# Behind four norms: the fourth tile's high-weight products move between the last input rows of the first three tiles, and the splits and the last sum around them change places

## The chip, the cores and the metric

One core of a Trainium2 chip runs the whole program. The metric is the device time of one execution in microseconds (us). TensorE (PE) does the matrix products, VectorE (DVE) and ScalarE (ACT) the elementwise work, GpSimd (POOL) a part of the gated product of the feed-forward layers, and SyncE (SP) starts the loads of the weights from memory.

## The reference, cut to what matters

Two networks run one after the other on 256 tokens (the first with 16 extra ones in front, so 272 columns) of width 1024. The first one has a gated DeltaNet layer and an mLSTM layer, each followed by a convolutional feed-forward layer; the second one has a mixed convolution and attention layer, a mixed linear and latent attention layer, and two SwiGLU layers. What surrounds the change is this part, which stands behind each mixer and each feed-forward layer of the first network:

```python
def rms_norm(x, w):
    xf = x.astype(jnp.float32)
    y = xf * lax.rsqrt(jnp.mean(xf * xf, -1, keepdims=True) + RMS_EPS)
    return (y * w.astype(jnp.float32)).astype(x.dtype)
...
    hs = hs + keep * rms_norm(mix, norm_w[i, 1])
    f = conv_ffn(rms_norm(hs, norm_w[i, 2]), ffn_w_up[i], ffn_conv_w[i], ffn_conv_b[i], ffn_w_down[i])
    hs = hs + keep * rms_norm(f, norm_w[i, 3])
```

So a layer's output is normalised and added to `hs`, the new `hs` is normalised again, and the result is multiplied by the next weight matrix (the feed-forward layer's `w_up`, or a mixer's `w_in`).

## The kernel before, in words

**Weights.** All weight matrices lie in one stream of 399 blocks that are split, plus a few that are used as they are. A block is 128 x 1024: for a matrix of the "tiles" kind it holds the weights that give one tile of 128 output rows, as eight 128 x 128 pieces, one for each of the eight 128-row pieces of the input (KC = 8). Four slots (`SLOTS`) hold four blocks. SP loads block n into `raw` once block n-4 has been split. ACT makes the high half `whi`, a copy rounded to fp32r (`split_hi`, line 394); it waits for the load, and for PE to be done with block n-4 (`block_used`). DVE makes the low half `wlo` = `raw` - `whi` (`split_lo`, line 399). The input is kept in the same way as a high part, `xs[:, k]`, and a low part, `xs[:, 8 + k]`. A product of the two is three matmuls: high weight by high input, high weight by low input, low weight by high input (`three`, lines 421, 422 and 423). An output tile takes 8 x 3 = 24 of them, all into one of eight banks.

**The wave.** Where a phase begins behind a norm, the input arrives row by row, so `pe_tiles` works on the first three tiles (`AHEAD` = 3) at once. For k = 0 to 7 it takes, as soon as the high part of row k is there, six matmuls (line 440 and 441: both weight halves of three blocks by the high input), and one step later three more with the low input of the row before (line 447). Then it goes on tile by tile with 24 matmuls each (`tile`), each tile behind a wait for its `wlo` and for its bank.

**The norm's scale.** The mean square of `hs` isn't needed for these products: each output is multiplied by the scale afterwards. ACT squares each row (line 735), DVE adds the squares in pairs and fours (`pair_sum`, `four_sum`, lines 688 and 694), and PE adds the two fours over the partitions with a matrix of ones (line 626, through `meanwhile`: `four3` within step 6 and `four7` within step 8, in both cases before the three matmuls of line 447). Then ACT takes the logarithm (`act_scale`, line 546) and the exponential (line 549): that is the scale. Between the two it splits the fifth block's high half. Its next instruction loads the function table of the next phase (lines 3175, 1848 and 3187), and only after it the high half of the sixth block is split. DVE's first instruction of the feed-forward phase multiplies tile 0 by the scale (line 862), and it then waits for that high half to make the sixth block's low half, before it comes to tile 1.

**The four places.** `pe_tiles` is called with such a wave behind `post0` (phase `up0`, 44 tiles of 272 columns), `post1` (`ml_in`, the mLSTM's first 13 tiles of 272 columns), `post2` (`up1`, 44 tiles of 258 columns) and `post3` (`ev_in`, six tiles of 256 columns). The last one begins the second network, which has no norm there, so it has no squares, no sum and no scale. `next_act` and `next_dve` are ACT's and DVE's part at the first three places, `last_act` and `last_dve` at the fourth. In front of each wave PE does 16 matmuls whose results nobody reads (`keep_clock`, line 617).

In the mLSTM phase DVE's first work behind the scale is the sixth block's low half and the two gate rows; ACT waits for these, and DVE waits for ACT again before it begins two scans over the tokens (lines 1875 and 1876), with products and low halves between their steps. PE waits for what comes of them (line 2162) before it goes on at line 1974.

**Order.** Every engine works through its own instructions in the order in which they are written; semaphores alone tie them together. The order within `next_dve` and `next_act` is written out by hand.

Of the kernel before, what the change touches and what calls it, by code (L numbers as in the profile page):

```python
# [21 lines left out]
P = 128  # L22
D = 1024
KC = D // P
N_META, SEQ = 16, 256
T1 = N_META + SEQ
# [27 lines left out]
SLOTS = 4  # L54
AHEAD = 3
# [230 lines left out]
def build(nc, stream, params, consts, mla, hs_in, out, table):  # L286
# [15 lines left out]
    whi_f, whi = shared("whi_f", [P, SLOTS, BLOCK], "whi", [P, SLOTS, BLOCK])  # L302
    wlo_f, wlo = shared("wlo_f", [P, SLOTS, BLOCK], "wlo", [P, SLOTS, BLOCK])
# [33 lines left out]
    def splits(n):  # L337
        return n + 1 - (len(PLAIN) if n >= PLAIN.stop else 0)
# [6 lines left out]
    hi_split = sem("hi_split")  # L345
# [43 lines left out]
    def split_hi(act, n, i=0):  # L389
        s = n % SLOTS  # L390
        act.wait_ge(block_loaded[s], i * (16 * 8 // SLOTS) + 16 * (n // SLOTS + 1))
        if n >= SLOTS:
            act.wait_ge(block_used, i * 8 + (n - SLOTS + 1))
        nc.scalar.activation(whi[:, s, :], raw[:, s, :], ACT.Copy).then_inc(hi_split, 1)  # L394

    def split_lo(dve, n, i=0):
        s = n % SLOTS
        dve.wait_ge(hi_split, i * 8 + splits(n))
        nc.vector.tensor_tensor(wlo[:, s, :], raw[:, s, :], whi[:, s, :].bitcast(F32), ALU.subtract).then_inc(block_split, 1)  # L399

    def fourth(phase):
        return FIRST_BLOCK[phase] + AHEAD

    def fifth(phase):
        return FIRST_BLOCK[phase] + AHEAD + 1
# [16 lines left out]
        nc.tensor.matmul(out_, whi[:, slot, w], lo, start=False, stop=False)  # L422
        return nc.tensor.matmul(out_, wlo[:, slot, w], hi, start=False, stop=stop)  # L423

    def pe_tiles(pe, phase, g0, name, count=None, meanwhile=lambda k: None):

        b0, n = FIRST_BLOCK[phase], count or COUNT[phase]
        T = cols(phase)
        mm = nc.tensor.matmul

        for k in range(KC + 1):
            if k < KC:
                w = slice(k * P, (k + 1) * P)
                pe.wait_ge(*S("norm", "act").at(f"{name}_hi{k}"))
                for j in range(AHEAD):
                    o, s = rhs_out(g0 + j, phase), (b0 + j) % SLOTS
                    if k == 0:
                        pe.wait_ge(block_split, splits(b0 + j))
                        pe.wait_ge(bank_free, g0 + j + 1)
                    mm(o, whi[:, s, w], xs[:, k, T], start=(k == 0), stop=False)  # L440
                    mm(o, wlo[:, s, w], xs[:, k, T], start=False, stop=False)  # L441
            if k:
                meanwhile(k - 1)
                w = slice((k - 1) * P, k * P)
                pe.wait_ge(*S("norm", "dve").at(f"{name}_lo{k - 1}"))
                for j in range(AHEAD):
                    last = mm(rhs_out(g0 + j, phase), whi[:, (b0 + j) % SLOTS, w], xs[:, KC + k - 1, T], start=False, stop=(k == KC))  # L447
                    if k == KC:
                        last.then_inc(block_used, 1)

        def tile(j, i=0):
            g = g0 + j
            pe.wait_ge(block_split, i * 8 + splits(b0 + j))
            pe.wait_ge(bank_free, i * 8 + (g + 1))
            for k in range(KC):
                last = three(rhs_out(g, phase), (b0 + j) % SLOTS, k, xs[:, k, T], xs[:, KC + k, T], k == 0, k == KC - 1)
            last.then_inc(block_used, 1)

        turns = (n - AHEAD) // 8
        if turns:  # L460
            with pe.Fori(0, turns) as i:
                for j in range(AHEAD, AHEAD + 8):
                    tile(j, i)
        for j in range(AHEAD + turns * 8, n):
            tile(j)

    def width(phase):
# [14 lines left out]
    def rhs_out(g, phase):  # L482
        return bank[g % 8][:, cols(phase)]
# [59 lines left out]
    def act_scale(act, name, g, dst, T, count, eps, lo=0, meanwhile=lambda: None):  # L543

        act.wait_ge(*S("norm", "pe").at(name))
        nc.scalar.activation(dst, bank[g % 8][:, lo:T], ACT.Ln, bias=eps, scale=1.0 / count).then_inc(bank_free, 1)
        meanwhile()
        act.wait_ge(bank_free, 8 + g + 1)
        nc.scalar.activation(dst, dst, ACT.Exp, scale=-0.5).then_inc(*S("norm", "act").mark(f"{name}_scale"))
# [134 lines left out]
    def pair_sum(dve, name, m, T, lo=0):  # L684

        v = S("norm", "dve")
        dve.wait_ge(*S("norm", "act").at(f"{name}_{m}"))
        nc.vector.tensor_tensor(sq[:, m, lo:T], sq[:, m - 1, lo:T], sq[:, m, lo:T], ALU.add).then_inc(*v.mark(f"{name}_pair{m}"))
# [19 lines left out]
    def next_dve(dve, post, name, row, phase):  # L708
        t = slice(PRE_FIRST[name], T1)

        def lo(m):
            dve.wait_ge(*S("norm", "act").at(f"{name}_hi{m}"))
            nc.vector.scalar_tensor_tensor(xs[:, KC + m, t], hs[:, m, t], pv("norm_w", row * KC + m), xs[:, m, t].bitcast(F32),
                                           ALU.mult, ALU.subtract).then_inc(*S("norm", "dve").mark(f"{name}_lo{m}"))

        for m in range(KC):
            add_y(dve, post, m)
            if m:
                lo(m - 1)
            if m % 2 == 0 and m:  # L720
                pair_sum(dve, name, m - 1, T1, t.start)
            if m == 5:
                four_sum(dve, name, 3, T1, t.start)
        lo(KC - 1)
        pair_sum(dve, name, KC - 1, T1, t.start)
        four_sum(dve, name, KC - 1, T1, t.start)
        split_lo(dve, fourth(phase))
        split_lo(dve, fifth(phase))

    def next_act(act, post, name, row, g, phase):  # L730
        t = slice(PRE_FIRST[name], T1)
        for m in range(KC):
            act.wait_ge(*S("norm", "dve").at(f"{post}_h{m}"))
            nc.scalar.activation(xs[:, m, t], hs[:, m, t], ACT.Copy, scale=pv("norm_w", row * KC + m)).then_inc(*S("norm", "act").mark(f"{name}_hi{m}"))  # L734
            nc.scalar.activation(sq[:, m, t], hs[:, m, t], ACT.Square).then_inc(*S("norm", "act").mark(f"{name}_{m}"))
            if m == 4:
                split_hi(act, fourth(phase))
        act_scale(act, name, g, rs[:, 0, t], T1, D, eps_1, t.start, lambda: split_hi(act, fifth(phase)))

    def last_dve(dve, post, name):  # L740

# [2519 lines left out]
    @block.tensor  # L3261
    def _(pe):
        first_pe(pe, "pre0", G["pre0"])
        pe.wait_ge(loaded, 16)
        gates_pe(pe, "gdn", G["gdn_g"], ((0, GROWS),), "gdn_gates", GROWS, T1, xk, lambda k: S("norm", "dve").at(f"pre0_x{k}"))
        pe_tiles(pe, "gdn_in", G["gdn_in"], "pre0", 32)
        gdn_pe(pe)
        in_wave = lambda name: fours_in_wave(pe, name, G[name], T1, PRE_FIRST[name])
        ln_wave = lambda n: fours_in_wave(pe, f"ln{n}v", G[f"lv{n}"], T2)
        pe_wide(pe, "gdn_out", G["gdn_out"], mix_ready("gdn"), gdn_banks_read, gdn_rows_between)  # L3270
        post_pe(pe, "post0", G["post0"])
        pe_tiles(pe, "up0", G["up0"], "pre1", None, in_wave("pre1"))
        pe_wide(pe, "down0", G["down0"], ffn_ready(0))
        post_pe(pe, "post1", G["post1"])
        pe_tiles(pe, "ml_in", G["ml_in"], "pre2", ML_FIRST, in_wave("pre2"))
        ml_pe(pe)
        pe_wide(pe, "ml_out", G["ml_out"], mix_ready("ml"), ml_banks_read)
        post_pe(pe, "post2", G["post2"])
        pe_tiles(pe, "up1", G["up1"], "pre3", None, in_wave("pre3"))
        pe_wide(pe, "down1", G["down1"], ffn_ready(1))  # L3280
        post_pe(pe, "post3", G["post3"])
        pe_tiles(pe, "ev_in", G["ev_in"], "b2", EV_FIRST)
        even_pe(pe)
        pe_wide(pe, "ev_out", G["ev_out"], mix_ready("ev"), even_banks_read)
        ln_pe(pe, 0)
        pe_tiles(pe, "up2", G["up2"], "ln0", None, ln_wave(0))
        pe_wide(pe, "down2", G["down2"], ffn_ready(2))
        ln_pe(pe, 1)
        pe_tiles(pe, "od_in", G["od_in"], "ln1", OD_FIRST, ln_wave(1))
        odd_pe(pe)  # L3290
        pe_wide(pe, "od_out", G["od_out"], mix_ready("od"), od_banks_read)
        ln_pe(pe, 2)
        pe_tiles(pe, "up3", G["up3"], "ln2", None, ln_wave(2))
        pe_wide(pe, "down3", G["down3"], ffn_ready(3))
        ln_pe(pe, 3)
        last_square = lambda m: ("act", f"ln3v_{m}", sqt(m))
        sums_pe(pe, "ln3v", last_square, G["lv3"], [(m, m == 0, m == KC - 1) for m in range(KC)], T2)
# [19 lines left out]
```

## Time and profile before

| | |
|---|---|
| median of 3 runs | 1497.07 us (1494.78 to 1497.19) |
| the profiled execution | 1497.1 us, of which 1495.2 us are the span from its first to its last instruction |
| PE, DVE, ACT, POOL busy | 98%, 69%, 52%, 18% of the span |
| the chain that ended last | 76% PE, 15% DVE, 4% ACT, 4% issue |
| matmuls of the three products on `xs` (lines 421 to 423) | 3 x 1976, some 285 ns each, overlapped |
| high halves on ACT, low halves on DVE | 399 each, 1056 ns and 1270 ns |
| table load on ACT | 1.28 us |

All times in views are microseconds from the span's start. Matmuls overlap: one of 272 columns is listed with some 0.29 us but the next one starts about 0.125 us after it, so PE's busy share says little of its slack, and the distance between starts is what counts. The time in brackets is idle time of the engine just before an instruction, and behind the arrow stands what ended it.

### The profile page before, as it was taken

How to read it: one execution, taken by the hardware profiler on the slowest of the kernel's cores; microseconds unless marked ns; L12 is line 12 of the kernel's file. 1: busy time of each engine (PE TensorE's matmuls, PEld its weight loads, DVE VectorE, ACT ScalarE, POOL GpSimd, SP SyncE). 2: the span in 40 equal slices, each digit the busy share in tenths (PEclk: the TensorE clock that was granted, in tenths of full speed). 3: DMA queues.
4: the chain of work that ended last, by engine and by line, in shares of the span. 5: the costliest groups of instructions: out<-in, count | busy, mean ns of one | idle time of the engine just before them, and what ended most of it. 6: DMA issues, size and time to landing. Idle time of an engine off the chain costs nothing.

```text
span 1495.2 us, 32391 instructions
## 1 busy us (share of the span) xinstructions
PE 1462.8 (98%) x11641; PEld 1395.3 (93%) x11641; DVE 1029.7 (69%) x1748; ACT 784.3 (52%) x1380; POOL 270.5 (18%) x308
## 2 busy tenths in 40 slices
PE   9999999999999999999999999999999999999997
PEld 7997877799999998899999998999999989999997
DVE  6884857658886468557888467677664696776654
ACT  6556324446655365456666356455553566554443
POOL 0203002102544000000554000013320012033300
PEclk9999999999999999999999999999999998999999
DMA  6551222154655535234665644546556523465551
GB/s 225 183 177 48 85 73 71 39 181 123 192 177 177 180 108 175 87 106 133 188 193 182 189 131 148 166 134 205 182 169 200 168 87 114 141 211 182 183 184 57
DMA packets 61141, 222.54 MB, mean 149 GB/s; under 512 B 6784, under 2 KB 7808, under 8 KB 60672
## 3 DMA queue, kind: packets, MB, share of 16 engines
q1 hardware_dynamic: 60912, 220.17, 46.7%
q8 instruction: 60, 0.98, 0.3%
q10 hardware_dynamic: 144, 1.18, 0.2%
q14 instruction: 25, 0.20, 0.0%
HBM read 220.28 MB, written 1.05 MB: 148 GB/s over the span
## 4 chain that ended last, share of the span: by engine, by line
PE 76%; DVE 15%; ACT 4%; issue 4%; DVEq 1%; DMA 1%; ACTq 0%; SPq 0%
PE bank L421 20%; PE bank L422 20%; PE bank L423 20%; DVE wlo L399 4%; PE bank L1069 2%; DVE bank L862 1%; PE bank L440 1%; PE bank L447 1%; PE bank L441 1%; ACT cv L768 1%; ACT whi L394 1%; PE bank L2003 1%; PE bank L626 1%; DVE cv L776 1%; DVE work L1673 1%
## 5 line engine op out<-in xcount | busy, mean ns | idle before, releaser
L399 DVE TENSOR_TENSOR wlo<-raw,whi 128x1024 fp32r<-128x1024 f32 x399 | 504.6, 1270 | 257.6 <-ACT whi L394 257.3
L421 PE MATMUL bank<-xs,whi 128*128 128x258 f32 (+2 forms) x1976 | 569.3, 288 | 3.6 <-DVE wlo L399 3.0
L394 ACT ACTIVATE whi<-raw 128x1024 fp32r<-128x1024 f32 x399 | 417.0, 1056 | 293.3 <-PE bank L423 276.9
L422 PE MATMUL bank<-xs,whi 128*128 128x258 f32 (+2 forms) x1976 | 564.1, 285 | 0.0
L423 PE MATMUL bank<-xs,wlo 128*128 128x258 f32 (+2 forms) x1976 | 561.7, 284 | 0.0
L421 PEld LDWEIGHTS bank<-xs,whi 128*128 128x128 f32 x1976 | 374.8, 190 | 9.0 <-issue 6.2
L423 PEld LDWEIGHTS bank<-xs,wlo 128*128 128x128 f32 x1976 | 375.5, 190 | 0.0
L422 PEld LDWEIGHTS bank<-xs,whi 128*128 128x128 f32 x1976 | 375.0, 190 | 0.4 <-issue 0.2
L421 PE MATMUL bank<-hf,whi 128*128 (+3 forms) x1024 | 291.0, 284 | 1.9 <-DVE cv L776 1.0
L423 PE MATMUL bank<-hf,wlo 128*128 (+3 forms) x1024 | 289.6, 283 | 0.0
L422 PE MATMUL bank<-hf,whi 128*128 (+3 forms) x1024 | 289.6, 283 | 0.0
L421 PEld LDWEIGHTS bank<-hf,whi 128*128 128x128 f32 x1024 | 192.6, 188 | 3.7 <-issue 1.7
L422 PEld LDWEIGHTS bank<-hf,whi 128*128 128x128 f32 x1024 | 192.9, 188 | 0.1
L423 PEld LDWEIGHTS bank<-hf,wlo 128*128 128x128 f32 x1024 | 192.8, 188 | 0.0
L776 DVE SCALAR_TENSOR_TENSOR cv<-bank,par,cv 128x271 f32<-128x271 f32 (+4 forms) x272 | 118.4, 486 | 33.5 <-ACT cv L768 33.3
L898 POOL CAST hf<-cv 128x256 f32 (+3 forms) x88 | 58.9, 669 | 378.1 <-DVE cv L874 370.5
L768 ACT ACTIVATE cv<-bank,par 128x272 f32<-128x272 f32 (+1 forms) x120 | 64.2, 548 | 100.7 <-DVE bank L862 81.3
L900 POOL TENSOR_TENSOR hf<-cv,hf 128x256 f32 (+3 forms) x88 | 101.7, 1156 | 16.6 <-POOL hf L898 15.4
L894 POOL TENSOR_TENSOR cv<-cv 128x272 f32<-128x272 f32 (+1 forms) x44 | 47.4, 1077 | 237.1 <-ACT cv L836 237.1
L862 DVE TENSOR_TENSOR bank<-bank,rs 128x256 f32<-128x256 f32 (+2 forms) x176 | 74.2, 430 | 11.5 <-PE bank L423 11.2
L440 PE MATMUL bank<-xs,whi 128*128 128x258 f32 (+2 forms) x192 | 52.7, 304 | 6.0 <-ACT xs L734 4.4
L841 ACT ACTIVATE head_v<-bank 128x1 f32<-128x1 f32 x88 | 14.9, 170 | 78.6 <-DVE bank L862 78.5
(473 smaller groups left out, 1548.5 us busy)
## 6 DMA issues: line engine op xcount, KB each, us to landing
raw<-stream SPq DMA_DIRECT2D x412, 512.0 KB, 3.6
con<-consts SPq DMA_DIRECT2D x1, 1284.5 KB, 11.0
big<-mla ACTq DMA_DIRECT2D x1, 1152.0 KB, 8.5
hs_sb<-hs SPq DMA_DIRECT2D x1, 1088.0 KB, 5.1
y_out<-hs_sb SPq DMA_DIRECT2D x8, 128.0 KB, 2.1
par<-params SPq DMA_DIRECT2D x1, 644.0 KB, 6.2
```

The lines of the kernel that those rows point to most:

```text
L394: nc.scalar.activation(whi[:, s, :], raw[:, s, :], ACT.Copy).then_inc(hi_split, 1)
L399: nc.vector.tensor_tensor(wlo[:, s, :], raw[:, s, :], whi[:, s, :].bitcast(F32), ALU.subtract).then_inc(block_split, 1)
L421: nc.tensor.matmul(out_, whi[:, slot, w], hi, start=start, stop=False)
L422: nc.tensor.matmul(out_, whi[:, slot, w], lo, start=False, stop=False)
L423: return nc.tensor.matmul(out_, wlo[:, slot, w], hi, start=False, stop=stop)
L440: mm(o, whi[:, s, w], xs[:, k, T], start=(k == 0), stop=False)
L768: nc.scalar.activation(cv[:, slot, lo:T1], bk[:, lo:T1], ACT.Identity, **args).then_inc(*steps_.mark(f"{tag}{a}"))
L776: ins = nc.vector.scalar_tensor_tensor(o[:, lo + tap:T1], bk[:, lo:T1 - tap], w[:, taps - 1 - tap:taps - tap], o[:, lo + tap:T1], ALU.mult ...
L862: nc.vector.tensor_tensor(u, u, rs[:, 0, FFN_FIRST[f]:T], ALU.mult).then_inc(*st.mark(f"u{f}_{base}_{j}{a}"))
L894: nc.gpsimd.tensor_tensor(h, cv[:, t2 % 8, t], h, ALU.mult).then_inc(*st.mark(f"h{f}_{base}_{j}"))
L898: nc.gpsimd.tensor_copy(hi, h).then_inc(*st.mark(f"hi{f}_{base}_{j}"))
L900: nc.gpsimd.tensor_tensor(lo, h, hi.bitcast(F32), ALU.subtract).then_inc(conv_taken, 2)
```

## The change

At the four places the fourth tile no longer comes behind the wave as 24 matmuls in one piece.

- PE: its 16 matmuls with the high weight half (two for each of the eight rows: high and low input) are set into the wave. Four stand in step 6 behind that step's six matmuls of line 440 and 441, four in step 7 at the same point, four at the head of step 8, and four behind step 8's matmuls of line 447. Then come the wait for the fourth block's low half and the eight matmuls with it, and then the last sum of squares, which before stood in step 8. The loop of whole tiles begins with the fifth tile.
- DVE (`next_dve`): the fourth block's low half is made before the last pair and four of squares, not after them.
- ACT (`next_act`): the fifth block's high half is made before the logarithm, not between logarithm and exponential.
- `ev_in` gets PE's part alone; `last_act` and `last_dve` stay as they are.

```diff
+    SOONER = {6: (0, 1), 7: (2, 3), 8: (4, 5)}
+
+    def pe_tiles(pe, phase, g0, name, count=None, meanwhile=lambda k: None, sooner=False):
...
+        done = AHEAD + 1 if sooner else AHEAD
+
+        def high_weights(c):
+            w, o, s = slice(c * P, (c + 1) * P), rhs_out(g0 + AHEAD, phase), (b0 + AHEAD) % SLOTS
+            mm(o, whi[:, s, w], xs[:, c, T], start=(c == 0), stop=False)
+            mm(o, whi[:, s, w], xs[:, KC + c, T], start=False, stop=False)
+
+        def low_weights(c):
+            w, o, s = slice(c * P, (c + 1) * P), rhs_out(g0 + AHEAD, phase), (b0 + AHEAD) % SLOTS
+            return mm(o, wlo[:, s, w], xs[:, c, T], start=False, stop=(c == KC - 1))
...
+            if sooner and k in SOONER:
+                if k == min(SOONER):
+                    pe.wait_ge(hi_split, splits(b0 + AHEAD))
+                    pe.wait_ge(bank_free, g0 + AHEAD + 1)
+                for c in SOONER[k]:
+                    high_weights(c)
             if k:
-                meanwhile(k - 1)
+                if k < KC or not sooner:
+                    meanwhile(k - 1)
...
+        if sooner:
+            for c in range(KC - 2, KC):
+                high_weights(c)
+            pe.wait_ge(block_split, splits(b0 + AHEAD))
+            for c in range(KC):
+                last = low_weights(c)
+            last.then_inc(block_used, 1)
+            meanwhile(KC - 1)
...
         lo(KC - 1)
+        split_lo(dve, fourth(phase))
         pair_sum(dve, name, KC - 1, T1, t.start)
         four_sum(dve, name, KC - 1, T1, t.start)
-        split_lo(dve, fourth(phase))
         split_lo(dve, fifth(phase))
...
-        act_scale(act, name, g, rs[:, 0, t], T1, D, eps_1, t.start, lambda: split_hi(act, fifth(phase)))
+        split_hi(act, fifth(phase))
+        act_scale(act, name, g, rs[:, 0, t], T1, D, eps_1, t.start)
...
-        pe_tiles(pe, "up0", G["up0"], "pre1", None, in_wave("pre1"))
+        pe_tiles(pe, "up0", G["up0"], "pre1", None, in_wave("pre1"), True)
...
-        pe_tiles(pe, "ev_in", G["ev_in"], "b2", EV_FIRST)
+        pe_tiles(pe, "ev_in", G["ev_in"], "b2", EV_FIRST, sooner=True)
```

## Rows read from the trace of the kernel before

**Rows 1.** The page's head and its line for PE: busy us, share, instructions.

```profile
span 1495.2 us, 32391 instructions
...
PE 1462.8 (98%) x11641; PEld 1395.3 (93%) x11641; DVE 1029.7 (69%) x1748; ACT 784.3 (52%) x1380; POOL 270.5 (18%) x308
```

**Rows 2.** The chain that ended last, start of `up0`: start, us, what.

```profile
349.00 0.42 ACT rs L549
349.44 1.28 ACT L3175
350.73 1.07 ACT whi L394
351.82 1.23 DVE wlo L399
...
359.44 1.23 DVE wlo L399
...
360.79 0.39 PE bank L421
```

**Rows 3.** Timeline of PE, last steps of the wave of `up0`: start, us.

```profile
343.78 0.39 PE L440 MATMUL bank<-xs,whi 128*128 128x272 f32 x1 [0.24 <-ACT xs L734]
...
345.54 0.39 PE L440 MATMUL bank<-xs,whi 128*128 128x272 f32 x1
345.77 0.29 PE L441 MATMUL bank<-xs,wlo 128*128 128x272 f32 x1
...
346.27 0.29 PE L441 MATMUL bank<-xs,wlo 128*128 128x272 f32 x1
...
346.90 0.72 PE L626 MATMUL bank<-sq,con 128*128 128x272 f32 x2
...
348.12 0.39 PE L421 MATMUL bank<-xs,whi 128*128 128x272 f32 x1
```

**Rows 4.** Timeline of ACT: `post0`'s logarithm and exponential, `pre1`'s logarithm.

```profile
332.97 0.49 ACT L648 ACTIVATE rs<-bank,con_eps 128x272 f32<-128x272 f32 x1 [0.56 <-PE bank L626]
333.49 0.43 ACT L650 ACTIVATE rs<-rs 128x272 f32<-128x272 f32 x1
...
347.67 0.49 ACT L546 ACTIVATE rs<-bank,con_eps 128x272 f32<-128x272 f32 x1 [1.86 <-PE bank L626]
```

**Rows 5.** Timeline of DVE: low halves of the fourth and the fifth block, `up0`.

```profile
346.76 1.22 DVE L399 TENSOR_TENSOR wlo<-raw,whi 128x1024 fp32r<-128x1024 f32 x1
349.13 1.23 DVE L399 TENSOR_TENSOR wlo<-raw,whi 128x1024 fp32r<-128x1024 f32 x1 [1.15 <-ACT whi L394]
```

**Rows 6.** The chain that ended last, start of `ml_in`.

```profile
557.03 0.42 ACT rs L549
...
566.15 0.30 DVE work L1907
```

**Rows 7.** Waits of PE, 540 to 600 us: us in total, times, longest.

```profile
PE bank L1974 <- DVE work L2162: 1.5, 1, 1.5
```

**Rows 8.** Timeline of PE, `up1`: two matmuls two places apart, and the eighth tile.

```profile
696.39 0.28 PE L440 MATMUL bank<-xs,whi 128*128 128x258 f32 x1
...
696.63 0.28 PE L440 MATMUL bank<-xs,whi 128*128 128x258 f32 x1
...
711.05 0.38 PE L421 MATMUL bank<-xs,whi 128*128 128x258 f32 x1 [0.60 <-DVE wlo L399]
```

**Rows 9.** Timelines of PE and ACT, end of `ev_in`'s wave.

```profile
893.92 0.87 PE L447 MATMUL bank<-xs,whi 128*128 128x256 f32 x6
894.71 0.39 PE L421 MATMUL bank<-xs,whi 128*128 128x256 f32 x1
...
894.66 1.06 ACT L394 ACTIVATE whi<-raw 128x1024 fp32r<-128x1024 f32 x1 [1.60 <-PE bank L447]
```

**Rows 10.** Stretches: length, busy us (instructions) of PE, PEld, DVE, ACT, POOL; granted clock.

```profile
590.69:597.52 6.83, 6.82 (x29) 6.27 (x30) 2.95 (x7) 0.65 (x2) 1.04 (x3) 0.52 0.71 229
914.96:918.37 3.41, 1.76 (x16) 1.55 (x15) 3.31 (x5) 1.33 (x2) 0.00 (x0) 1.00 0.42 145
```

More of the change, by code:

```diff
@@ L423, in three @@
         return nc.tensor.matmul(out_, wlo[:, slot, w], hi, start=False, stop=stop)
-    def pe_tiles(pe, phase, g0, name, count=None, meanwhile=lambda k: None):
+    SOONER = {6: (0, 1), 7: (2, 3), 8: (4, 5)}
+    def pe_tiles(pe, phase, g0, name, count=None, meanwhile=lambda k: None, sooner=False):
         b0, n = FIRST_BLOCK[phase], count or COUNT[phase]
@@ L457, in tile @@
             last.then_inc(block_used, 1)
-        turns = (n - AHEAD) // 8
+        turns = (n - done) // 8
         if turns:
             with pe.Fori(0, turns) as i:
-                for j in range(AHEAD, AHEAD + 8):
+                for j in range(done, done + 8):
                     tile(j, i)
-        for j in range(AHEAD + turns * 8, n):
+        for j in range(done + turns * 8, n):
             tile(j)
@@ L3271, in _ @@
         post_pe(pe, "post0", G["post0"])
-        pe_tiles(pe, "up0", G["up0"], "pre1", None, in_wave("pre1"))
+        pe_tiles(pe, "up0", G["up0"], "pre1", None, in_wave("pre1"), True)
         pe_wide(pe, "down0", G["down0"], ffn_ready(0))
         post_pe(pe, "post1", G["post1"])
-        pe_tiles(pe, "ml_in", G["ml_in"], "pre2", ML_FIRST, in_wave("pre2"))
+        pe_tiles(pe, "ml_in", G["ml_in"], "pre2", ML_FIRST, in_wave("pre2"), True)
         ml_pe(pe)
@@ L3278, in _ @@
         post_pe(pe, "post2", G["post2"])
-        pe_tiles(pe, "up1", G["up1"], "pre3", None, in_wave("pre3"))
+        pe_tiles(pe, "up1", G["up1"], "pre3", None, in_wave("pre3"), True)
         pe_wide(pe, "down1", G["down1"], ffn_ready(1))
         post_pe(pe, "post3", G["post3"])
-        pe_tiles(pe, "ev_in", G["ev_in"], "b2", EV_FIRST)
+        pe_tiles(pe, "ev_in", G["ev_in"], "b2", EV_FIRST, sooner=True)
         even_pe(pe)
```

## Prediction

> **What bounds the kernel now.** I read the page first. PE is busy for 98% of the span [rows 1], and nearly all of it is weight products whose number the change leaves alone. So the time can move only where PE stands still or starts something late, and I looked at the four places for that: PE's timeline for its idle times, then ACT's and DVE's for what ended them, then the chain that ended last for what follows from them.
>
> In `up0` the wave's last steps run from 343.78 to 348.12. Starts of matmuls of 272 columns lie 0.125 us apart (five starts from 345.77 to 346.27), with about 0.1 us more behind the first one after a wait (345.54 to 345.77). The sum of squares starts at 346.90, and behind it the fourth tile at 348.12 [rows 3]. Up to the sum there is hardly any idle time: the sum itself waits some 0.1 us for `four7`. Behind it the fourth tile waits for its low half, which DVE makes only from 346.76 [rows 5]; three matmuls behind the sum would have let it start some 0.5 us earlier. So what can be filled is about 0.6 us in a stage with a norm.
>
> The chain shows something heavier. It doesn't run through the fourth tile but through the scale: exponential at 349.00, table load at 349.44, the sixth block's high half at 350.73, its low half at 351.82, then scaled tiles, convolutions and low halves in turn on DVE and ACT, until the low half that starts at 359.44 lets PE begin the eighth tile at 360.79 [rows 2]. PE was idle before that start, so at the eighth tile this chain has no slack at all. None of its members waits for PE: the tiles that DVE scales in it had long been finished. Whatever delays the exponential delays the eighth tile by as much, and afterwards PE is bound again and has no way to catch up.
>
> **The change part by part.** Count the matmuls from the start of step 6's six to the last sum. Before: 6 + 3 + 6 + 3 = 18. After: 6 + 4 + 3 + 6 + 4 + 3 + 4 + 3 + 4 + 8 = 45. The other sum is in both. The 27 more cost 27 x 0.125 = 3.4 us; the 0.1 us that the sum waited for `four7` is filled, and about the same is added for first matmuls behind waits. So the sum starts 3.4 us later, at about 350.3, and the logarithm, 0.77 us behind it as now (346.90 to 347.67), at 351.1 [rows 3, 4].
>
> From logarithm to exponential it is 1.33 us now, because a high half lies between. With that taken out it is what it is in the norm before, where nothing stands between them: 333.49 - 332.97 = 0.52 us [rows 4]. So the exponential comes 3.4 - 1.33 + 0.52 = 2.6 us later, at 351.6. Moving the high half gives back 0.8 of the 3.4.
>
> Behind the exponential nothing is changed: table load, high half and low half of the sixth block. The low half ends at 353.05 now and at 355.6 then. PE would want the sixth tile at about 354 (348.12 and two tiles of 24 x 0.125 + 0.1), so PE stands for some 1.6 us there, again before the seventh, and the eighth tile starts at 360.79 + 2.6 = 363.4. The stalls are not added to the 2.6; they are how it shows.
>
> The other moves are covered. The fourth block's low half, moved before the last pair and four, ends at about 347.2 on DVE; PE wants it behind 37 of the 45 matmuls, after 349 (346.90 and 19 x 0.125). The pair and four come 1.1 us later, to about 348, and the sum wants them at 350.3. The fourth tile's high half is ready and its bank free before step 6, the one made just after row 4's square, the other freed by DVE's fifth bank read. The fifth block's high half waits for the first block to be used, now behind 12 more matmuls; its halves end at about 351 instead of 350.3, and PE wants that tile at 350.8: 0.1 to 0.3 us, which the wait for the sixth swallows. No load is issued from a new place; SP's load of block n+4 follows the split of block n, so those behind the sixth move with it.
>
> A rule that speaks against the change: the Trainium skill, page "TensorE: Matmul & The Clock Gate", section "Step-by-step: what each phase is for", says that TensorE may pull weight loads forward but that "the MATMULs themselves stay in program order". The trace agrees: in step 8 three matmuls with their input ready stand behind the waiting sum [rows 3]. If PE could let the ready sum pass the eight low products, each stage with a norm would lose 8 x 0.125 = 1.0 us less; by the rule it doesn't.
>
> In `ml_in` the columns and the order are the same, so 2.6 us again. Its exponential stands at 557.03 in the chain, which goes on through the sixth block's halves and the gate rows between ACT and DVE to 566.15 [rows 6] and then through DVE's scans, in one piece without idle time, until PE, after 1.5 us of waiting, starts line 1974 [rows 7]. No cover there either: 2.6.
>
> In `up1` two starts lie 0.24 us apart for two matmuls, 0.12 each [rows 8], so 27 x 0.12 = 3.2 and 3.2 - 1.33 + 0.52 = 2.4 us. The eighth tile waits 0.60 us for its low half as before [rows 8], so all of it is paid: 2.4.
>
> In `ev_in` there is no sum and no scale. The first three tiles' last low products are six matmuls from 893.92, so the first tile ends its use with the fourth of them, and ACT starts the fifth block's high half 0.4 us later, at 894.66. With 12 matmuls before it this is 12 x 0.12 = 1.4 us later, less about 0.1 of idle time filled: 896.0. High half 1.06, low half 1.2 [rows 5, 9]: 898.3, plus 0.1 to PE. Before, the fifth tile followed the fourth at 894.71 + 24 x 0.12 + 0.1 = 897.7. So 0.7 us lost, where at most 0.1 could be won: the fourth tile's wait here is next to nothing.
>
> Sum: 2.6 + 2.6 + 2.4 + 0.7 = 8.3 us on a span of 1495.2. The profiled execution took 1.9 us more than its span, 1497.1, which is also the median: 1497.1 + 8.3 = 1505.4 us.
>
> Bounds of what the trace doesn't show. First, how many matmuls behind a satisfied wait start 0.1 us late: none to four more in a stage, so 0 to +0.4 us each, from the 0.23 against 0.125 of rows 3; I take one. Second, the distance from logarithm to exponential: 0.49, the logarithm's own length, to 0.52 [rows 4]; I take the latter, which has the same wait. Third, the clock, below.
>
> **The rivals.** (1) Late scale, paid in full, as above: 1503 to 1507.
>
> (2) The clock falls as well. Behind an idle time with only small matmuls ahead of it PE was granted 0.52 on average for 6.83 us in the mLSTM, which is the lower level, 1.2 GHz; in `ev_in`'s phase a stretch with 1.76 of 3.41 us busy kept 1.00 [rows 10]. My new gap of 1.6 us between dense tiles is nearer to the second, so I think it holds. If it fell, the sixth or seventh tile would take twice its 3 us for a while. Much of that hides in the waits for the seventh and eighth tile, so it costs 0.1 to 1.7 us in each of three stages: 1506 to 1510. The mLSTM's own fall could also lengthen, by up to half its 6.83, 3.4 us.
>
> (3) The delay is partly caught up. If DVE and ACT ran the chain to the eighth tile faster than I think, for instance because a low half and a scaling changed their waits, 1 us in a stage would come back: 1500 to 1503. Against it speaks that every piece of the chain is already without idle time for PE's sake.
>
> (4) Not slower: the scale is off the path and only the filled idle time counts. It decides if the exponential may be late by more than 2.6 us without PE waiting. For the sixth tile the room is 354.2 - 353.1 = 1.1 us, which speaks for a little cover; for the eighth it is below zero, since PE waits there already. If it held, three stages would win 0.5 us each and `ev_in` 0.1: 1497.1 - 1.6 = 1495.5. Only with the mLSTM's low clock gone too (half of 6.83 us) would it be 1492, faster by more than 0.2%.
>
> (5) The change doesn't do what it says, since a moved matmul waits for something unexpected, the fourth bank say: the wave's high rows would start late, and the time would be above (1). I count it with (2).
>
> **How the numbers follow.** (1) 0.68, (2) and (5) 0.14, (3) 0.09, (4) 0.09, of which 0.03 with the clock's help. The predicted time is that of (1): 1505.4. The range of 8 in 10 leaves out (4) and the ends of (2) and (3): 1501 to 1509. A difference of 0.2% is 3.0 us, about what a measurement of this kernel can tell from none. Slower by more: all of (1), (2) and most of (3), 0.88. Within it: the rest of (3) and most of (4), 0.09. Faster: 0.03.
>
> **What would show it.** In `up0` the last line 626 near 350.3, behind the eight low products, not 346.9; logarithm and exponential 0.5 us apart, the latter near 351.6; idle time before the sixth tile of about 1.6 us ended by a low half, and the eighth tile at 363.4. In `ml_in` line 1974 2.6 us later relative to the wave's start, in `up1` the eighth tile 2.4 us later, in `ev_in` an idle time of 0.7 us before the fifth tile. The granted clock stays 1.00 in the three gaps. I am wrong if the exponential is late and the eighth tile isn't, or if `four7`'s sum starts before the low products are through.

## The result, and the profile after

Over 20 executions each the changed kernel's median is 1500.20 us (1495.18 to 1503.90) and before's 1495.38 (1490.93 to 1499.06): ratio 1.0038, 95% interval 1.0027 to 1.0049. It is slower, on the side that was forecast. As a difference it lies inside the range: 4.8 us, where 1501 to 1509 on a base of 1497.1 meant 3.9 to 11.9. As an absolute time it lies 0.8 us below 1501, since the three executions of before that were shown first (1497.07) lay high in its spread.

Times of one kernel spread over 8 us here, so the two profiled executions can't be subtracted as they stand (1498.3 against 1495.2 us). Their stages can. First the engines' line of the changed kernel's page: busy us, share, instructions.

```profile
PE 1458.3 (97%) x11641; PEld 1388.5 (93%) x11641; DVE 1029.9 (69%) x1748; ACT 785.4 (52%) x1380; POOL 270.7 (18%) x308
```

The same 11641 matmuls as in [rows 1]; only their order and their waits differ. Below is PE's timeline at the end of `up0`'s wave (start, us, what). Line numbers have moved: 452 is the old 440, 466 the old 447, 653 the old 626; 441 is now the eight low-weight products of the fourth tile.

```profile
346.86 0.40 PE L452 MATMUL bank<-xs,whi 128*128 128x272 f32 x1 [0.23 <-ACT xs L761]
...
352.08 1.16 PE L441 MATMUL bank<-xs,wlo 128*128 128x272 f32 x8
353.08 0.62 PE L653 MATMUL bank<-sq,con 128*128 128x272 f32 x2
354.03 0.39 PE L421 MATMUL bank<-xs,whi 128*128 128x272 f32 x1 [0.33 <-DVE wlo L399]
```

This execution is 3.1 us later than before's at the start of step 6 (346.86 against 343.78 in [rows 3]), so all times are read as distances from there. The last sum starts 6.22 us behind it, where it was 346.90 - 343.78 = 3.12. The fifth tile, though, starts at 7.17, and it was some 7.4: PE does win 0.3 us up to there. The squares for the sum were ready on DVE at 351.06, two microseconds earlier; it stood behind the products in front of it. (Step 6 itself isn't late: it is 8.22 us behind the wave's first matmul in both kernels.) ACT shows what the late sum does (timeline; logarithm and exponential are lines 573 and 576 now):

```profile
351.58 1.06 ACT L394 ACTIVATE whi<-raw 128x1024 fp32r<-128x1024 f32 x1 [2.69 <-PE bank L466]
353.74 0.49 ACT L573 ACTIVATE rs<-bank,con_eps 128x272 f32<-128x272 f32 x1 [1.10 <-PE bank L653]
354.26 0.43 ACT L576 ACTIVATE rs<-rs 128x272 f32<-128x272 f32 x1
```

The exponential stands 354.26 - 346.86 = 7.40 us behind the start of step 6, and stood at 349.00 - 343.78 = 5.22 [rows 2, 3]: 2.18 late. The chain that ended last runs on from it through the same members as in [rows 2] (start, us, what; L3203 is the table load, 1.28 us long, of which this view puts the larger part down to "issue"):

```profile
354.71 0.51 ACT L3203
...
356.00 1.07 ACT whi L394
357.10 1.23 DVE wlo L399
...
364.73 1.23 DVE wlo L399
...
366.07 0.39 PE bank L421
```

From the exponential to the eighth tile it is 11.81 us here and 11.79 before [rows 2]. Nothing is absorbed: the eighth tile is 19.21 us behind step 6 where it was 17.01, 2.20 late. On the way PE stands 1.16 us before the sixth tile, 0.54 before the seventh and 0.56 before the eighth. `ml_in` and `up1` show the same. PE's waits in `ml_in`'s stretch (us in total, times, longest):

```profile
PE bank L421 <- DVE wlo L399: 2.8, 5, 1.2
PE bank L2002 <- DVE work L2190: 1.5, 1, 1.5
```

The wait of 1.5 us before the old line 1974 is as long as in [rows 7], and its end has moved: 41.08 us behind step 6 (557.08 to 598.16), where it was 38.88. The waits of whole tiles for low halves are 2.8 us in five; in before they are 0.4 us in two. In `ev_in` (PE's timeline; step 6, fifth tile):

```profile
898.33 0.36 PE L452 MATMUL bank<-xs,whi 128*128 128x256 f32 x1
...
904.70 0.39 PE L421 MATMUL bank<-xs,whi 128*128 128x256 f32 x1 [0.82 <-DVE wlo L399]
```

The fourth tile is through, and the fifth has to wait 0.82 us for its low half, where it followed without a wait. The distance is 6.37 us instead of 5.80.

**Where the other 4 us went.** The stages lost 2.2 + 2.2 + 2.0 + 0.6 = 7.0 us and this execution is 3.1 longer. Between them lies the clock. Columns as in [rows 10]; first a stretch of before, then three of the changed kernel, then one of the run of before against itself (below).

```profile
1240.00:1260.00 20.00, 18.46 (x239) 17.80 (x238) 11.69 (x22) 10.02 (x19) 5.99 (x6) 0.74 0.43 136
```

```profile
120.00:136.00 16.00, 15.79 (x74) 9.79 (x72) 4.33 (x14) 5.15 (x18) 0.47 (x2) 0.79 0.10 33
596.00:605.00 9.00, 7.50 (x56) 6.73 (x55) 6.74 (x14) 3.62 (x9) 1.05 (x3) 1.00 0.76 235
1240.00:1260.00 20.00, 18.44 (x280) 17.89 (x279) 16.61 (x34) 13.76 (x28) 9.49 (x9) 1.00 0.49 159
```

```profile
1240.00:1260.00 20.00, 18.22 (x262) 17.22 (x261) 12.80 (x27) 15.19 (x33) 4.25 (x5) 1.00 0.47 161
```

PE was granted the lower level, 1.2 GHz, for 6.8 us in the mLSTM of before [rows 10] and not at all in that of the changed kernel, behind the same wait of 1.5 us; the changed kernel had such a stretch near 130 us (74 matmuls in 16 us where before had 96, at 1.00), which before had not. These two cost 3.4 us each and cancel. The third doesn't: behind a wait of 1.5 us at 1245 before lost 20 x 0.26 = 5.2 us to the lower level, while the changed kernel and the other execution of before went through the same stretch at 1.00. The mean clocks, 0.992 and 0.995, give 12.0 and 7.5 us lost (one minus the clock, times the span): a difference of 4.5. So for every execution below I also give the **time with the clock taken out**: its time less its span times one minus its mean granted clock. The clock is listed to 0.001, which is 1.5 us in a single execution and averages out over many. That leaves some 0.7 us of uncertainty in any one execution; the distances lie in stretches that were granted 1.00 and don't depend on it.

### The profile page after: what moved, and what is told of

Same layout as the page of the kernel before. It is cut to its first block, busy times and chain, and to the rows that moved or that the text cites. A ratio compares the mean times of both kernels' runs of the same rounds, so it can differ in the third digit from the quotient of the medians.

```text
span 1498.3 us, 32391 instructions
## 1 busy us (share of the span) xinstructions
PE 1458.3 (97%) x11641; PEld 1388.5 (93%) x11641; DVE 1029.9 (69%) x1748; ACT 785.4 (52%) x1380; POOL 270.7 (18%) x308
## 4 chain that ended last, share of the span: by engine, by line
PE 75%; DVE 15%; ACT 5%; issue 4%; DVEq 1%; DMA 0%; ACTq 0%
PE bank L421 19%; PE bank L422 19%; PE bank L423 19%; DVE wlo L399 5%; PE bank L1097 2%; DVE bank L890 1%; PE bank L452 1%; ACT whi L394 1%; PE bank L466 1%; PE bank L453 1%; ACT cv L796 1%; PE bank L2031 1%; DVE cv L804 1%; PE bank L653 1%; DVE work L1701 1%
## 5 line engine op out<-in xcount | busy, mean ns | idle before, releaser
L421 PE MATMUL bank<-xs,whi 128*128 128x258 f32 (+2 forms) x1944 | 558.3, 287 | 10.8 <-DVE wlo L399 10.7
L422 PE MATMUL bank<-xs,whi 128*128 128x258 f32 (+2 forms) x1944 | 553.0, 284 | 0.0
L423 PE MATMUL bank<-xs,wlo 128*128 128x258 f32 (+2 forms) x1944 | 550.6, 283 | 0.0
L421 PEld LDWEIGHTS bank<-xs,whi 128*128 128x128 f32 x1944 | 366.6, 189 | 18.0 <-issue 11.9
L423 PEld LDWEIGHTS bank<-xs,wlo 128*128 128x128 f32 x1944 | 367.4, 189 | 0.0
L422 PEld LDWEIGHTS bank<-xs,whi 128*128 128x128 f32 x1944 | 366.8, 189 | 0.4 <-issue 0.2
L452 PE MATMUL bank<-xs,whi 128*128 128x258 f32 (+2 forms) x192 | 52.4, 301 | 6.0 <-ACT xs L761 4.4
```

What stands on the lines that cost most here:

```text
L421: nc.tensor.matmul(out_, whi[:, slot, w], hi, start=start, stop=False)
```

## The experiments

Distances are those above: from the start of step 6 to the eighth tile (`up0`, `up1`), to the old line 1974 (`ml_in`) and to the fifth tile (`ev_in`), each less before's 17.01, 16.70, 38.88 and 5.80. "Clock out" is the mean with the clock taken out, with its standard error, less before's: 79 executions of three series on two chips, whose means lie within 0.2 us of each other. (The 20 executions of before beside the changed kernel's first 20 have no clock on record.)

| kernel | ratio (95%) | `up0` | `ml_in` | `up1` | `ev_in` | sum | clock out |
|---|---|---|---|---|---|---|---|
| before, unchanged | 0.9993 (0.9983 to 1.0003) | 0.0 | 0.0 | 0.0 | 0.0 | 0.0 | +0.3 (0.2) |
| changed, first 20 | 1.0038 (1.0027 to 1.0049) | +2.2 | +2.2 | +2.0 | +0.6 | +7.0 | +7.2 (0.2) |
| changed again | 1.0046 (1.0029 to 1.0063) | +2.2 | +2.2 | +2.0 | +0.6 | +7.0 | +7.0 (0.4) |
| sum back in step 8 | 1.0025 (1.0012 to 1.0038) | +1.5 | +1.5 | +1.5 | +0.6 | +5.0 | +5.4 (0.3) |
| sum and split back | 1.0033 (1.0020 to 1.0047) | +1.1 | +1.2 | +1.1 | +0.6 | +4.0 | +3.5 (0.2) |
| late sum alone | 1.0070 (1.0050 to 1.0090) | +3.3 | +3.3 | +3.2 | 0 | +9.8 | +9.6 (0.4) |
| `ev_in` back | 1.0050 (1.0034 to 1.0066) | +2.2 | +2.2 | +2.0 | 0.0 | +6.4 | +6.0 (0.1) |
| high products behind the sum | 0.9992 (0.9981 to 1.0004) | 0.0 | 0.0 | 0.0 | -0.2 | -0.2 | -0.3 (0.1) |
| the same, table load later | 0.9983 (0.9974 to 0.9992) | -0.9 | -0.5 | -1.2 | -0.2 | -2.9 | -3.0 (0.2) |
| before, table load later | 0.9983 (0.9970 to 0.9997) | -0.6 | -0.5 | -0.9 | 0.0 | -2.0 | -2.5 (0.2) |
| changed, table load later | 1.0032 (1.0019 to 1.0044) | +0.9 | +1.7 | +0.7 | +0.6 | +3.8 | +3.7 (0.1) |

Before's own level is 1485.4 us with the clock taken out (79 executions, 1484.3 to 1487.1), while its times as measured run from 1490.7 to 1499.5.

**Before against itself.** No edit.

> The kernel before, unchanged, timed against itself. The changed kernel's profiled execution was 3.1 us longer than before's, but its stages at the four places lost 2.2 + 2.2 + 2.0 + 0.6 = 7.0 us. Theory A (clock): the difference is low-clock time, which falls in different places in every execution, so this kernel, against itself, shows times that spread by some 5 us or more and follow the mean granted clock (0.001 of it worth about 1.5 us), at a ratio of 1.000, with marks within a stage at the same distances as in before to 0.1 us. Theory B: the 4 us come back somewhere in the program through the change itself; then this kernel's times spread by under 1.5 us and don't follow the clock.

The marks lie at the same distances to 0.02 us. The twelve executions spread over 5.1 us and their median is 2.5 us below that of before in the same series, with nothing changed. Over the 79 executions of before a thousandth of the mean clock goes with 1.33 us (correlation -0.97). Theory A holds: what was missing between 7.0 and 3.1 us is the clock's draw, most of it the stretch at 1240 to 1260, which this execution of the same kernel doesn't have. (A full 1.5 us for each thousandth, as the table takes out, is a little more than 1.33; for mean clocks at most 0.0011 apart, as here, that is under 0.2 us.)

**The last sum back in step 8.**

```diff
-                if k < KC or not sooner:
-                    meanwhile(k - 1)
+                meanwhile(k - 1)
...
             last.then_inc(block_used, 1)
-            meanwhile(KC - 1)
```

> The changed kernel with the last sum of squares back inside step 8, ahead of the three matmuls of line 466 (the old line 447), in the three stages with a norm. The fourth tile's high-weight products and the moved splits stay. Late-scale theory: 12 matmuls still stand before the sum, so it starts some 1.3 us later than before the change and not 3.1; the fifth block's high half now ends after the sum and holds the logarithm back, so exponential and eighth tile come 1.6 us later than before instead of 2.2: 3 x 0.6 = 2 us less than the changed kernel. Rival (the loss comes from the 16 products among the rows, not from the sum): nothing comes back, and the eighth tile stays 2.2 us late.

0.7, 0.7 and 0.5 us came back in the three stages. In `up0` the sum now starts 4.34 us behind step 6, 1.22 later than before; the logarithm comes only at 6.17, behind the fifth block's high half, and the exponential at 6.67, 1.45 late. The eighth tile is 1.47 late.

**Sum and fifth split back.** In addition:

```diff
-        split_hi(act, fifth(phase))
-        act_scale(act, name, g, rs[:, 0, t], T1, D, eps_1, t.start)
+        act_scale(act, name, g, rs[:, 0, t], T1, D, eps_1, t.start, lambda: split_hi(act, fifth(phase)))
```

> As the run with the sum back in step 8, and the fifth block's high half again between logarithm and exponential. Late-scale theory: sum and logarithm 1.3 us later than before the change, exponential 1.33 us behind the logarithm again, eighth tile 1.3 us late instead of 2.2: 3 x 0.9 = 2.7 us less than the changed kernel. Rival (the split ahead of the logarithm is what saves time): eighth tile later than in the run with the sum back alone.

1.1 to 1.2 late instead of 1.3. What is left is the 12 matmuls: 1.5 us of work, of which 0.3 fills idle time, so the sum is 1.22 late and the exponential (6.35 behind step 6) 1.13.

**The late sum alone.** The kernel before, with the fourth tile whole and behind the wave:

```diff
-                meanwhile(k - 1)
+                if k < KC or not later:
+                    meanwhile(k - 1)
...
+        if later:
+            tile(AHEAD)
+            meanwhile(KC - 1)
+            done = AHEAD + 1
...
-        act_scale(act, name, g, rs[:, 0, t], T1, D, eps_1, t.start, lambda: split_hi(act, fifth(phase)))
+        split_hi(act, fifth(phase))
+        act_scale(act, name, g, rs[:, 0, t], T1, D, eps_1, t.start)
```

> The kernel before, with the fourth tile as 24 matmuls in one piece behind the wave and DVE's order as it was, but the last sum of squares moved behind that whole tile, and the fifth block's high half ahead of the logarithm, in the three stages with a norm; ev_in as before. Late-scale theory: the sum comes 27 matmuls and the 0.5 us wait for the fourth low half later, 3.9 us, less 0.1 for its own old wait; the exponential 3.8 - 1.33 + 0.52 = 3.0 us later; the eighth tile 3.0 us late in up0 and ml_in's line 1974 too, 2.8 in up1: 8.8 us slower than before (1.0059), although no product was moved. Rival (the scale is off the path, the loss comes from the products among the rows): within 1 us of before.

No product stands in the wave here, and the kernel is slower than the changed one. PE's timeline in `up0` (step 6, then the eighth tile):

```profile
344.68 0.39 PE L440 MATMUL bank<-xs,whi 128*128 128x272 f32 x1 [0.23 <-ACT xs L740]
...
365.01 0.39 PE L421 MATMUL bank<-xs,whi 128*128 128x272 f32 x1 [0.55 <-DVE wlo L399]
```

The eighth tile is 20.33 us behind step 6, 3.3 late where 3.0 was expected. This is the run that separates the two causes: a late scale is enough by itself. The rival, that the moved products cost the time, is ruled out as the main cause. From the exponential to the eighth tile of `up0` it is 11.80 us here, as in every kernel so far (11.79 to 11.81), though the exponential stands anywhere from 5.21 to 8.53 us behind step 6; to the old line 1974 of `ml_in` it is 33.7 us in all of them.

**`ev_in` back.** The changed kernel with `pe_tiles(pe, "ev_in", G["ev_in"], "b2", EV_FIRST)` as it was.

> The changed kernel with ev_in as before (its fourth tile in one piece behind the wave); the three stages with a norm stay changed. Late-split theory: the fifth tile of ev_in no longer waits 0.8 us for its low half, and the way from step 6 to the fifth tile is 0.6 us shorter: 0.6 us less than the changed kernel, the other three stages 2.2, 2.2 and 2.0 us late as in it. Rival (filling the wave wins something in ev_in and hides it later): no idle time goes, or the time rises.

The fifth tile is back at 5.78 us and its wait is gone. With the clock taken out it is some 1.1 us below the changed kernel, where 0.6 was expected; as measured it looks slower than it (medians 1501.20 and 1500.53 in one series), so the rival is answered by the distance, and by the total only once the clock is taken out.

**The high products in one piece behind step 8.** Sum and splits as before the change; only the order within the fourth tile differs from before (16 with the high half, then the wait for the low half, then eight).

```diff
-            for c in range(KC - 2, KC):
-                high_weights(c)
+            pe.wait_ge(hi_split, splits(b0 + AHEAD))
+            pe.wait_ge(bank_free, g0 + AHEAD + 1)
+            for c in range(KC):
+                high_weights(c)
```

> The fourth tile's 16 high-weight matmuls in one piece behind step 8, its eight low-weight ones behind them, the last sum in step 8, and ACT's and DVE's order as before the change: nothing is added ahead of the sum. Late-scale theory: exponential and eighth tile stand where they stood before the change, to 0.1 us; the fourth tile no longer waits 0.4 to 0.5 us for its low half, but the eighth waits that much longer, so the time is before's (1.000, within 0.3 us once the clock is taken out). Rival (idle time of PE filled is time won): 0.4 us less in each of the four stages, 1.6 us faster.

Step 6 (line 451 here) and the eighth tile of `up0`, PE's timeline:

```profile
346.56 0.39 PE L451 MATMUL bank<-xs,whi 128*128 128x272 f32 x1 [0.24 <-ACT xs L754]
...
363.58 0.39 PE L421 MATMUL bank<-xs,whi 128*128 128x272 f32 x1 [0.56 <-DVE wlo L399]
```

17.02 us, as before. The fifth tile starts 0.4 us sooner and the eighth one waits longer for it. The idle time that the change set out to fill is real, and filling it gives nothing in the stages with a norm, since DVE's and ACT's chain sets the eighth tile. In `ev_in`, where no scale is waited for, the same edit won 0.2 us.

**The table load behind the sixth high half.** The same kernel with one more edit; in `ml_in` the two gate rows' copies go ahead of the load too.

```diff
         act_scale(act, name, g, rs[:, 0, t], T1, D, eps_1, t.start, lambda: split_hi(act, fifth(phase)))
+        split_hi(act, fifth(phase) + 1)
...
-            if f < 2 and first_pair(i, t):
-                split_hi(act, b0 + FFN_TAIL, ii)
```

> As the run with the high products behind the sum, and in the three stages with a norm the sixth block's high half moved ahead of ACT's table load (in ml_in the two gate rows' copies too). Late-scale theory: the chain from the exponential to the eighth tile gets shorter by the part of the table load that isn't needed, 1.1 us: the eighth tile of up0 and up1 starts 0.9 us earlier than before the change (then PE itself bounds it), ml_in's line 1974 1.3 us earlier; together 3 us faster than before, 0.998. Rival (the chain is not what bounds PE): nothing is won over the run before it.

ACT's timeline in `up0` shows the high half in front of the load, 0.3 us behind the exponential's start at 348.78, and PE's (step 6, eighth tile) what it does:

```profile
349.10 1.05 ACT L394 ACTIVATE whi<-raw 128x1024 fp32r<-128x1024 f32 x1
350.17 1.28 ACT L3193 ACT_TABLE_LOAD   x1
```

```profile
343.56 0.39 PE L451 MATMUL bank<-xs,whi 128*128 128x272 f32 x1 [0.24 <-ACT xs L754]
...
359.64 0.29 PE L421 MATMUL bank<-xs,whi 128*128 128x272 f32 x1
```

16.08 us, 0.93 less than before, and without a wait. `ml_in` gave 0.5 and not 1.3: the seventh high half, which stands behind the gate rows' copies, now comes before ACT can go on with them (559.14, then the gate rows at 560.11 in this execution). The whole is 3.0 us below before with the clock taken out, and 0.9983 as measured. This version is faster than both kernels.

**The table load alone, on before and on the changed kernel.**

> The kernel before with one edit: in the three stages with a norm the sixth block's high half ahead of ACT's table load (in ml_in the gate rows' copies too). Chain theory: the eighth tile no longer waits for its low half, so up0 and up1 win the 0.5 us and 0.7 us that PE stood there, and not the 0.4 us before the fourth tile; ml_in's line 1974 0.5 us earlier as in the run with both edits: 1.7 us less than before with the clock taken out, where both edits gave 3.0. Rival (the table load is hidden in any case): nothing.

The eighth tile of `up0` came 0.56 us sooner, the time that PE had lost before it, and `ml_in`'s line 0.54. `up1` gave 0.9. The distances add up to 2.0 us and the time with the clock taken out says 2.5; both are above the 1.7 expected, and the last half microsecond I can't place. Together with the run before this one: filling the fourth tile's wait begins to pay once the chain is out of the way (2.9 against 2.0 us by the distances; 3.0 against 2.5, each with an error of 0.2, by the times).

> The changed kernel with the same edit of the table load. Chain theory: with the scale 2.2 us late the chain bounds PE from the sixth tile to the eighth, so what is taken out of the chain, 1.1 us, comes back in full in up0 and up1, and 0.5 us in ml_in: 2.7 us less than the changed kernel with the clock taken out, 4.4 above before. Rival (the 2.2 us come from the 16 matmuls on PE): only the 0.6 us of idle time in front of one tile could go, in each stage.

The eighth tile of `up0` is 0.9 us late and not 2.2, that of `up1` 0.7 and not 2.0: 1.3 came back in each, where 1.1 was expected, for the whole table load of 1.28 us has left the chain (10.51 us from the exponential to the eighth tile of `up0`). The total is 3.5 us below the changed kernel and not 2.7; the sum of the four distances, 3.8, is the 3.7 measured. The rival had its idle time too small: before the sixth tile the changed kernel loses 1.3 us, so this run by itself doesn't rule it out. The late sum alone does, where nothing stands in the wave.

**The changed kernel again.**

> The changed kernel once more, on another chip beside before. Clock theory: with the low-clock time taken out (the time less the span times one minus the mean granted clock) it is 7.2 us above before, as in the first 20 runs; uncorrected it lies 4 to 9 us above, by the luck of the draw. If the changed kernel truly loses less clock than before, its mean granted clock is again 0.001 above before's and the uncorrected difference again under 6 us.

7.0 us with the clock taken out, and 7.0 between the medians too, where the second sign asked for under 6. Its mean clock is 0.9947 again, over 26 executions 0.9948 with a standard error of 0.0004, and before's is 0.9942 with 0.0002: whether the changed kernel gets 0.8 us back through the clock stays open.

## Why the prediction was right

**What bounds** was read rightly: the chain from the exponential had no slack at the eighth tile. It is 11.8 us long before and after, and a late scale, filled idle time and a shortened chain, each tried alone, moved the eighth tile as this says. Only `ml_in`'s chain was read too simply, as DVE's scans in one piece: in before's execution a weight load of 3.40 us (from 584.79) stands near its end. The load starts behind a low half of the same chain, so it moved with it.

**The mechanism's price** was too high by 1.3 of 8.3 us, in two terms. The 27 matmuls ahead of the sum were put at 3.4 us, after setting off 0.1 against 0.1; the sum came 3.1 later (3.12 to 6.22). The 0.1 us charged for a first matmul behind a wait didn't come, and more idle time was filled than counted. Before, the first one of step 7 started 0.06 us late and had a slow start (0.23 to the next one [rows 3]); after, with products ahead of it, it follows at once and the next start comes at 0.13, so 0.16 is won there, besides the 0.1 before the sum. And the logarithm came 0.66 us behind the sum's start, not 0.77. With exponential minus logarithm at 0.52, as forecast, this makes 2.2, 2.2 and 2.0 instead of 2.6, 2.6 and 2.4.

**`ev_in`** lost 0.6 us for 0.7, in the way described: the fifth block's high half, which waits for the first tile, starts 4.00 us behind step 6 where it was 2.81, and the fifth tile waits 0.82 us (0.7 forecast).

**The covers held.** The fourth low half and the pair and four were ready in time, and the fifth tile waited 0.33 us (0.1 to 0.3 forecast) and still started 0.3 sooner than before. The sixth waited 1.16 us and not 1.6: the scale was 0.4 less late than forecast.

**The rivals.** (2), a clock that falls in the new gaps, didn't come: it stayed at 1.00 in the 25 us behind step 6 at all four places, in each profiled execution with the changed wave's gaps. (3), a partial recovery, is ruled out by the equal length of the chain, and (4) by the run with the late sum alone and the one with the idle time filled alone. (5), a moved matmul held up, didn't come: in `up0` the first of them follows step 6's products at 0.13 us.

**The absolute time** is 5 us above the median that came. 1.3 is the price above. 1.7 is the base, the median of the three times shown against that of 20 (1497.07, 1495.38). The last 2.2 is the difference between the 7.0 us of the distances and the 4.8 between the medians, which is the clock's draw. I took the profiled execution as a fixed point and named the clock only as a risk of the change. It was the larger part of the uncertainty with or without it: against 1497.1 the range was 0.26% to 0.80% slower, which the measured 0.38% meets near its lower end, while the median itself fell below 1501.

## What to carry to other kernels

A reduction whose result only scales outputs can look like spare work; follow the chain from it before putting matmuls ahead of it. If PE waits for that chain anywhere later, each matmul ahead of the reduction costs its 0.125 us, less only the idle time that it fills there, and what fills idle time elsewhere earns nothing. Shorten the chain first: here one split moved ahead of a table load won 2.0 to 2.5 us, and only then did the filled wait pay.

Where times spread more than the change is worth, compare distances within a stage, and take the granted clock out of the total. Both gave 7 us here from executions whose medians differed by 4.8.

## What the runs showed of the hardware

In one and the same kernel the low clock comes in some executions and not in others. Behind a wait of 1.5 us before was granted 0.74 from 1240 to 1260 us in one execution and 1.00 in another; behind the 1.5 us wait in the mLSTM 0.82 and 0.91 (586 to 605 us). The times of before, 1490.7 to 1499.5, follow the mean clock, a thousandth of it for 1.33 us; with the clock taken out 2.8 us of spread are left.

The first matmul of 272 columns after idle time takes 0.23 us to the next start instead of 0.125 (343.78 to 344.01 in before). Behind a wait that has been satisfied for a while it mostly doesn't (0.13 in step 7 of the changed kernel). Where the input came only just ahead it can show without idle time: in step 4 of the changed kernel the high input is ready at 343.49, the matmul follows its predecessor in its normal place at 343.55, and the next one starts at 343.78.

The table load, 1.28 us, stands between its neighbours on ACT with 0.02 us or less on either side: 349.44 to 350.72 in before, behind an exponential that ends at 349.42 and ahead of a high half that starts at 350.73.
